# A transformer kernel on one core: a full weight slab ahead of the narrow one, and four smaller moves

## The chip, the cores and the metric

The kernel runs on one core of a Trainium2 chip. TensorE (PE) multiplies, VectorE (DVE), ScalarE (ACT) and GpSimd (POOL) do the rest, SyncE (SP) issues most DMAs. Each engine works off its own list of instructions in order; semaphores tie the lists together. The metric is the device time of one launch in microseconds; lower is better.

## The reference

One launch computes two transformer blocks one after the other on 256 rows of 1024 numbers, in float32:

```python
mod = silu(c) @ w_ada + b_ada                     # 6 vectors of 1024
h = rmsnorm(x, norm_mix_g) * (1 + sc_m) + sh_m
q, k, v, qi, ki, wi, u, ga, gb = split(h @ w_in)  # 5192 columns; ki 64, wi 8
y_attn = dsa_attention(q, k, v, qi, ki, wi) @ w_attn_proj   # top 64 keys by an index score
y_conv = conformer_conv(u, ...) @ w_conv_proj
x = x + g_m * ((sigmoid(ga) * y_attn + sigmoid(gb) * y_conv) @ w_out)
h = rmsnorm(x, norm_ffn_g) * (1 + sc_f) + sh_f
a, b = split(h @ w_ffn_in)
x = rmsnorm(x + g_f * ((silu(a) * b) @ w_ffn_out))
# second block: two attentions on h @ w_in_2, a cross attention to mem_2, a feed-forward
```

## The kernel before

**Weights.** A matmul of float32 is made of three in a rounded type: with w = w_hi + w_lo and a = a_hi + a_lo, it takes a_hi·w_hi, a_hi·w_lo and a_lo·w_hi (`mm3`, L527 to L529). SP loads weights in blocks of 1 MB into a ring of four (`load`, L390). A block is two pieces; ACT rounds each into w_hi (L1127) and DVE makes w_lo (L1551), again in a ring of four pieces. A slab of 512 output columns takes four pieces of 12 matmuls of 128x512, 48 in all. Numbers P_... count pieces, U_... count slabs (units), which alternate between PSUM banks 0, 1 and 2, 3. Before a block is loaded over an old one, SP waits until the last piece of the old one (`last_piece_of`) has its w_lo.

**The start.** POOL loads w_ada in 12 slabs of two 1 MB blocks (L478; the first four into `ada_raw` and `ada_start`); DVE multiplies each row group by silu(c) and sums (`ada_ops`, L1614 and L1617, eight instructions a slab). PE adds over the partitions (L618, one column each). With four slabs shift and scale of the first norm are known (L1636, `gain1` L1638). Between slabs DVE does the small steps of the first norm: the mean of the squares after slab 0 (`mean`, L1559), the scaled row group 0 after slab 1 (`rows0`, L1563), the copy of the transposed gain vectors and taps after slab 2 (L1630, L1631). POOL takes the power -1/2 (`rstd`, L484), ACT squares and scales row group 1. PE transposes the scaled rows (`turn`, L580), ACT and DVE apply gain and shift to two of four pairs of feature tiles each (L1155, L1576), then ACT rounds the four pairs into a_hi (L1161), then DVE makes a_lo (L1584).

**The first projection.** Its first slab is a narrow one, 72 columns (ki and wi; piece 0, block 0 of 288 KB), which waits for all four a_lo. Ten full slabs follow, pieces 1 on; DVE does slabs 4 to 11 of w_ada between their weight conversions, and the index scores, the top-64 search and the taps of the convolution. ki is copied twice side by side (`ki2`), transposed by PE after piece (1, 1) and moved by ACT.

**The norm before the first feed-forward** (`N_H2`): DVE adds the gated projection to x (L1952, L1957) by halves of 512 columns, ACT squares whole row groups (L1140), then mean, power, scaled rows, transposes and `features` as above.

**The second attention** ("b_"): 16 steps; at step n PE transposes probabilities (L733), issues the scores of step n + 2 (L724), does `mixed_step(n)`, a piece of 12 matmuls of another projection, then the values (L740). In `mixed_step` 5 and 6 it also transposes two groups of the memory's keys into bank 7 (L975); before the second it waits for DVE's copy of the first (`mem_kT`, L1602), which stands in DVE's step 8, the copy of the second in step 9.

## Time and profile before

| | us |
|---|---|
| runs of the kernel before (3) | 1026.27, 1028.21, 1029.89 |
| the profiled execution, its own time | 1027.91 |
| its span | 1026.1 |

| engine | busy us | share |
|---|---|---|
| PE matmul | 932.5 | 91% |
| PE weight load | 734.8 | 72% |
| DVE | 625.0 | 61% |
| ACT | 451.4 | 44% |
| POOL | 29.7 | 3% |

Stretches are in microseconds from the span's start. A timeline row has start and duration, engine, line of the program, operation, output<-input with shapes and the count of merged instructions; in brackets the idle time before it and what ended it. PEclk is the granted TensorE clock as a share of 2.4 GHz.

### The profile page before, as it was taken

How to read it: one execution, taken by the hardware profiler on the slowest of the kernel's cores; microseconds unless marked ns; L12 is line 12 of the kernel's file. 1: busy time of each engine (PE TensorE's matmuls, PEld its weight loads, DVE VectorE, ACT ScalarE, POOL GpSimd, SP SyncE). 2: the span in 40 equal slices, each digit the busy share in tenths (PEclk: the TensorE clock that was granted, in tenths of full speed). 3: DMA queues.
4: the chain of work that ended last, by engine and by line, in shares of the span. 5: the costliest groups of instructions: out<-in, count | busy, mean ns of one | idle time of the engine just before them, and what ended most of it. 6: DMA issues, size and time to landing. Idle time of an engine off the chain costs nothing.

```text
span 1026.1 us, 11727 instructions
## 1 busy us (share of the span) xinstructions
PE 932.5 (91%) x4133; PEld 734.8 (72%) x4133; DVE 625.0 (61%) x1015; ACT 451.4 (44%) x696; POOL 29.7 (3%) x41
## 2 busy tenths in 40 slices
PE   0599989998979999999999899797998899999997
PEld 0587544576868888887888678576777678888885
DVE  4868799857455555676766333577463555555544
ACT  1234222455354444543645434464254455555432
POOL 2101000000000000000000000000000000000000
PEclk9789999999889999999999989899999999999999
DMA  9959552446355655575554323145352346655541
GB/s 325 369 197 341 185 185 82 158 157 217 110 200 181 193 179 189 170 276 187 196 196 164 123 83 124 42 174 176 122 189 70 108 146 196 192 178 190 167 161 41
DMA packets 102853, 178.02 MB, mean 173 GB/s; under 512 B 6286, under 2 KB 52475, under 8 KB 102810
## 3 DMA queue, kind: packets, MB, share of 16 engines
q1 hardware_dynamic: 95994, 151.23, 44.9%
q0 software_dynamic: 6816, 26.22, 7.0%
q8 instruction: 26, 0.43, 0.2%
q14 instruction: 17, 0.14, 0.0%
HBM read 176.39 MB, written 1.05 MB: 173 GB/s over the span
## 4 chain that ended last, share of the span: by engine, by line
PE 76%; DVE 9%; issue 9%; ACT 3%; DMA 2%; POOL 0%; DVEq 0%; POOLq 0%; ACTq 0%
PE bank L527 19%; PE bank L529 18%; PE bank L528 18%; PE bank L879 9%; PE bank L560 3%; DVE conv_out L1763 2%; DVE ada_acc L1617 2%; ACT w_hi L1127 2%; DMA ada_raw<-in_w_ada 1%; PE bank L724 1%; DMA x_residual<-in_x 1%; PE bank L858 1%; PE bank L601 1%; PE bank L740 1%; DVE w_lo L1551 1%
## 5 line engine op out<-in xcount | busy, mean ns | idle before, releaser
L1551 DVE TENSOR_TENSOR w_lo<-raw_weights,w_hi 128x1024 fp32r<-128x1024 f32 (+1 forms) x259 | 315.0, 1222 | 283.1 <-ACT w_hi L1127 282.7
L1127 ACT ACTIVATE w_hi<-raw_weights 128x1024 fp32r<-128x1024 f32 (+1 forms) x259 | 272.4, 1058 | 334.4 <-PE bank L529 253.5
L527 PE MATMUL bank<-w_hi,a_hi 128*128 128x512 f32 (+1 forms) x792 | 322.2, 407 | 13.2 <-DVE a_lo L1584 5.6
L529 PE MATMUL bank<-w_hi,a_lo 128*128 128x512 f32 (+1 forms) x792 | 314.8, 397 | 0.0
L528 PE MATMUL bank<-w_lo,a_hi 128*128 128x512 f32 (+1 forms) x792 | 314.7, 397 | 0.0
L527 PEld LDWEIGHTS bank<-w_hi,a_hi 128*128 128x128 f32 x792 | 154.9, 196 | 49.1 <-issue 15.7
L529 PEld LDWEIGHTS bank<-w_hi,a_lo 128*128 128x128 f32 x792 | 154.6, 195 | 32.5
L528 PEld LDWEIGHTS bank<-w_lo,a_hi 128*128 128x128 f32 x792 | 155.2, 196 | 30.0 <-issue 0.2
L560 PE MATMUL bank<-raw_weights,feature_rows_early 128*128 128x512 f32 x144 | 68.0, 618 | 0.4 <-ACT z_projected L1201 0.4
L879 PE MATMUL bank<-w_hi,ff_hi 128*128 128x512 f32 x176 | 55.1, 394 | 0.8 <-DVE hidden_rows L2030 0.5
L879 PE MATMUL bank<-w_lo,ff_hi 128*128 128x512 f32 x176 | 54.3, 390 | 0.0
L879 PE MATMUL bank<-w_hi,ff_lo 128*128 128x512 f32 x176 | 54.2, 389 | 0.0
L1763 DVE SCALAR_TENSOR_TENSOR conv_out<-conv_in,conv_taps_T,conv_out 128x256 f32<-128x256 f32 x120 | 50.9, 475 | 0.0
L560 PEld LDWEIGHTS bank<-raw_weights,feature_rows_early 128*128 128x128 f32 x144 | 26.8, 195 | 32.0 <-issue 31.5
L1212 ACT ACTIVATE probabilities<-masked_scores,row_stats 128x128 f32<-128x128 f32 (+1 forms) x32 | 14.6, 455 | 59.8 <-DVE row_stats L1876 40.2
L879 PEld LDWEIGHTS bank<-w_hi,ff_hi 128*128 128x128 f32 x176 | 32.7, 188 | 8.6 <-DVE hidden_rows L2030 0.9
L879 PEld LDWEIGHTS bank<-w_hi,ff_lo 128*128 128x128 f32 x176 | 33.0, 188 | 7.0
L879 PEld LDWEIGHTS bank<-w_lo,ff_hi 128*128 128x128 f32 x176 | 33.0, 188 | 6.9
L1617 DVE SCALAR_TENSOR_TENSOR ada_acc<-ada_raw,row_stats,ada_acc 128x512 f32<-128x512 f32 x42 | 31.5, 750 | 3.2 <-DMA ada_raw<-in_w_ada 2.0
L527 PE MATMUL bank<-w_hi,mem_hi 128*128 128x512 f32 x64 | 26.3, 411 | 0.4 <-ACT z_projected L1235 0.4
L608 PE MATMUL bank<-constants,vector_rows 109*128 109x109 f32 x1 | 0.4, 416 | 28.2 <-DMA tap_rows<-in_w_dw 28.2
L529 PE MATMUL bank<-w_hi,mem_lo 128*128 128x512 f32 x64 | 25.7, 401 | 0.0
(244 smaller groups left out, 835.2 us busy)
## 6 DMA issues: line engine op xcount, KB each, us to landing
raw_weights<-in_w_in SPq DMA_DIRECT2D x40, 1024.0 KB, 5.1
raw_weights<-in_w_ffn_in SPq DMA_DIRECT2D x44, 512.0 KB, 4.7
raw_weights<-in_w_gate_up SPq DMA_DIRECT2D x44, 512.0 KB, 4.6
ada_raw<-in_w_ada POOLq DMA_DIRECT2D x12, 1024.0 KB, 8.1
raw_weights<-in_w_ffn_out SPq DMA_DIRECT2D x9, 1024.0 KB, 5.0
...
```

What stands on the lines that cost most here:

```text
L527: pe.matmul(ps, hi[:, kt, ts], wh, start=start, stop=False)
L528: pe.matmul(ps, hi[:, kt, ts], wl, start=False, stop=False)
L529: return pe.matmul(ps, lo[:, kt, ts], wh, start=False, stop=stop)
L560: last = pe.matmul(ps, f_h1[:, kt, t * P:(t + 1) * P], w, start=(kt == 0), stop=(kt == 2 * n - 1))
L601: last = pe.transpose(bank[b0 + g][:, kk * SEQ + t * P:kk * SEQ + (t + 1) * P], src[:, t, c:c + P], ident)
L724: pe.matmul(bank[4 + n % 2][:, 0:keys], q[half, h // 2, t * P:(t + 1) * P], k[half, h // 2, 0:keys], start=True, stop=True).then_inc(event ...
L879: o = pe.matmul(bank[out_bank(t, c)][:], lhs[:, kt, ts], w[:, c * W:(c + 1) * W], start=(kt == 0 and n == 0), stop=(kt == KF - 1 and n == 2))
L1127: act.activation(w_hi[:, slot, 0:m], raw[:, b % RAW, half * PIECE:half * PIECE + m], ACT.Copy)\
L1212: act.activation(p_work[:, n % 2, 0, 0:keys], s_work[:, n % 2, 0, 0:keys], ACT.Exp, scale=-1.0, bias=stat[:, 32 + n % 2:33 + n % 2], accum ...
L1551: dve.tensor_tensor(w_lo[:, slot, 0:m], raw[:, b % RAW, half * PIECE:half * PIECE + m], w_hi[:, slot, 0:m], ALU.subtract).then_inc(lo_read ...
L1617: o = dve.scalar_tensor_tensor(out=slot, in0=w, scalar=c, in1=slot, op0=ALU.mult, op1=ALU.add)
L1763: dve.scalar_tensor_tensor(out=conv_out[:, g, :], in0=conv_in[:, g, k:k + SEQ], scalar=taps[:, g, k:k + 1], in1=conv_out[:, g, :], op0=ALU ...
```

## The change

1. The first full slab of w_in (columns of u) becomes pieces 0 to 3 in blocks 0 and 1, and the narrow slab piece 4 in block 2. SP issues the loads after step 20 of w_ada's sums and not after 16. PE's first piece waits for its own pair of features only. ACT rounds two pieces before the features; DVE makes one residue of weights before them.
2. DVE takes the mean of the first norm after slab 1 of w_ada (before: slab 0), scales row group 0 after slab 2 (before: 1), and copies the vectors after slab 3 (before: 2), out of bank 3 and no longer 7. PE transposes the scaled rows before the vectors. The ki copies, transposes and move come one piece or more later.
3. `features`: ACT does pair 0 and rounds it, then pair 2, then rounds 1 to 3; DVE does pair 1, residue 0, pair 3, residues 1 to 3.
4. At N_H2 ACT squares halves of 512 columns as they come; DVE adds the two sums.
5. The table of constants is loaded in two parts: ident, ones and half ahead (264 of 1416 columns), the others after load 3; index scores and ln_mean wait for them.
6. Second attention: PE's key transposes in steps 5 and 8 (before 5 and 6), DVE's copies in steps 8 and 11 (before 8 and 9).

```diff
+    parts["half"] = np.full((P, KD), -0.5)
...
+P_FIRST, U_FIRST = 0, 0
+P_SMALL, U_SMALL = 4, 1
...
-    return (0, 0) if p == P_SMALL else (1 + (p - 1) // 2, (p - 1) % 2)
+    return (p // 2, p % 2) if p <= P_SMALL else (1 + (p - 1) // 2, (p - 1) % 2)
...
-    return 2 * b
+    return 2 * b + (b < 2)
@@ SP
-        sp.dma_start(const[:], const_dram[:]).then_inc(sem["const_landed"], 16)
+        early = cols["half"][1]
+        sp.dma_start(const[:, 0:early], const_dram[:, 0:early]).then_inc(sem["const_landed"], 16)
...
-        sp.wait_ge(ada_step, 16)
-        load(0, w2["w_in"].rearrange("(k p) n -> p k n", p=P)[:, :, C_KI:C_U], "small")
-        for s, c in enumerate(IN1_COLS):
+        sp.wait_ge(ada_step, 20)
+        for j in range(2):
+            load(j, slab_src(w2["w_in"], 4 * j, IN1_COLS[0]))
+        load(2, w2["w_in"].rearrange("(k p) n -> p k n", p=P)[:, :, C_KI:C_U], "small")
+        load(3, slab_src(w2["w_in"], 0, IN1_COLS[1]))
+        sp.dma_start(const[:, early:], const_dram[:, early:]).then_inc(sem["shapes_landed"], 16)
+        load(4, slab_src(w2["w_in"], 4, IN1_COLS[1]))
+        for s, c in enumerate(IN1_COLS[2:]):
             for j in range(2):
-                load(1 + 2 * s + j, slab_src(w2["w_in"], 4 * j, c))
+                load(5 + 2 * s + j, slab_src(w2["w_in"], 4 * j, c))
@@ PE
         pe.wait_ge(sem["const_landed"], 16)
+        turn(N_H1, xs_z)
         pe.wait_ge(small_landed, 16 * 12)
-        pe.transpose(bank[7][:, 0:V_ROWS], vec_rows[0:V_ROWS, :], ident[0:V_ROWS, 0:V_ROWS])
+        pe.transpose(bank[3][:, 0:V_ROWS], vec_rows[0:V_ROWS, :], ident[0:V_ROWS, 0:V_ROWS])
...
-        pe.wait_ge(sem["vec_copied"], 2)
-        turn(N_H1, xs_z)
...
         last.then_inc(sem["ada_reduced"], 1)
+        for j in range(4):
+            piece(P_FIRST + j, U_FIRST, j, 4, norm=N_H1)
+
+        pe.wait_ge(lo_ready, P_SMALL + 1)
         pe.wait_ge(sem["mod_copied"], 1)
-
-        pe.wait_ge(lo_ready, P_SMALL + 1)
-        pe.wait_ge(nt["lo"], 4 * F_OF[N_H1] + 4)
+        pe.wait_ge(sem["vec_copied"], 2)
...
-        for s in range(6):
+        for s in range(1, 6):
...
-                if (s, j) == (1, 1):
+                if (s, j) == (1, 2):
...
-            if 5 <= n < 7:
-                g = n - 5
+            if n in (5, 8):
+                g = n // 8
@@ ACT, features
+            affine(0)
+            rounded(0)
+            affine(2)
+            for g in range(1, 4):
+                rounded(g)
...
-        conv(P_SMALL)
+        conv(P_FIRST, 2)
         act.wait_ge(sem["gains"], 1)
         features(N_H1, f_h1, gain1, modT[:, 0:8])
-        conv(P_IN1, 3)
...
+        conv(P_FIRST + 2, 2)
...
+        conv(P_SMALL, 4)
+        slab_out(P_FIRST + 3, U_FIRST, IN1_COLS[0], ACT.Copy)
+        conv(P_SMALL + 4)
...
-        sumsq(N_H2, x, xs_u, updated(U_OUT1 + 2), {1: (P_FI1 + 1, 1)})
+        def half_squares(t, c, done):
+            act.wait_ge(acc_free[t], U_OUT1 + c + 1)
+            o = act.activation(xs_u[:, t, c * W:(c + 1) * W], x[:, t, c * W:(c + 1) * W], ACT.Square, scale=1.0 / 32,
+                               accum_out=d_stat[:, 28 + 2 * c + t:29 + 2 * c + t])
...
+        half_squares(0, 0, False)
+        half_squares(1, 0, False)
+        half_squares(0, 1, True)
+        conv(P_FI1 + 1)
+        half_squares(1, 1, True)
@@ DVE, features
+            affine(1)
+            residue(0)
+            affine(3)
+            for g in range(1, 4):
+                residue(g)
...
-            if s == 0:
+            if s == 1:
                 mean(N_H1)
-            elif s == 1:
+            elif s == 2:
                 rows0(N_H1, x, xs_z)
-            elif s == 2:
-                dve.wait_ge(sem["vec_turned"], 1)
...
+        dve.wait_ge(sem["vec_turned"], 1)
...
-        features(N_H1, f_h1, gain1, modT[:, 0:8], P_SMALL)
-        conv(P_IN1, 4)
+        conv(P_FIRST)
+        features(N_H1, f_h1, gain1, modT[:, 0:8])
+        conv(P_FIRST + 1, 3)
...
+            dve.wait_ge(sem["shapes_landed"], 16)
...
+        conv(P_SMALL)
...
-                if (s, k) == (0, 1):
+                if (s, k) == (1, 0):
...
-        mean(N_H2)
+        dve.wait_ge(nt["sumsq"], TT * (N_H2 + 1))
+        dve.scalar_tensor_tensor(out=stat[:, 2:4], in0=d_stat[:, 28:30], scalar=EPS, in1=d_stat[:, 30:32],
+                                 op0=ALU.add, op1=ALU.add).then_inc(nt["mean"], 1)
...
-            if 8 <= n < 10:
-                g = n - 6
+            if n in (8, 11):
+                g = 2 + n // 11
```

## Rows read from the trace of the kernel before

**Rows 1.** The page: busy time of the engines, GB/s in 40 slices, the chain.

```profile
PE 932.5 (91%) x4133; PEld 734.8 (72%) x4133; DVE 625.0 (61%) x1015; ACT 451.4 (44%) x696; POOL 29.7 (3%) x41
...
GB/s 325 369 197 341 185 185 82 158 157 217 110 200 181 193 179 189 170 276 187 196 196 164 123 83 124 42 174 176 122 189 70 108 146 196 192 178 190 167 161 41
...
PE 76%; DVE 9%; issue 9%; ACT 3%; DMA 2%; POOL 0%; DVEq 0%; POOLq 0%; ACTq 0%
```

**Rows 2.** Stretches: length, busy PE, PEld, DVE, ACT, POOL, clock, DMA share, GB/s.

```profile
46.30:56.50 10.20, 10.19 (x48) 10.20 (x49) 3.36 (x3) 1.96 (x3) 0.00 (x0) 0.50 0.67 240
56.50:61.30 4.80, 4.80 (x13) 3.82 (x13) 2.38 (x3) 1.18 (x2) 0.00 (x0) 0.50 0.20 35
61.30:69.80 8.50, 8.50 (x39) 6.98 (x38) 6.73 (x12) 3.18 (x3) 0.75 (x1) 1.00 0.55 187
69.80:120.00 50.20, 49.48 (x221) 36.23 (x219) 40.15 (x71) 19.99 (x34) 5.25 (x7) 1.00 0.77 279
120.00:200.00 80.00, 75.73 (x234) 37.56 (x234) 79.09 (x224) 21.10 (x54) 2.04 (x3) 0.96 0.44 146
```

**Rows 3.** Timeline of the start.

```profile
19.74 0.17 DVE L1559 TENSOR_SCALAR row_stats<-row_stats 128x2 f32<-128x2 f32 x1 [6.31 <-ACT scaled_rows_early L1140]
...
20.33 5.54 DVE L1617 SCALAR_TENSOR_TENSOR ada_acc<-ada_start,row_stats,ada_acc 128x512 f32<-128x512 f32 x7
...
36.51 3.12 DVE L1617 SCALAR_TENSOR_TENSOR ada_acc<-ada_start,row_stats,ada_acc 128x512 f32<-128x512 f32 x4 [0.65 <-DMA ada_start<-in_w_ada]
...
41.19 1.90 DVE L1576 TENSOR_SCALAR feature_rows_early<-bank,gain_h,modulation_T 128x256 f32<-128x256 f32 x4
...
43.67 2.50 DVE L1584 TENSOR_TENSOR a_lo<-feature_rows_early,a_hi 128x512 fp32r<-128x512 f32 x4
...
46.31 0.40 PE L527 MATMUL bank<-w_hi,a_hi 128*128 128x72 f32 x1 [5.58 <-DVE a_lo L1584]
```

**Rows 4.** Chain of waits: start, duration, 16 transposes at full clock.

```profile
492.88 1.75 PE bank L590 x16
```

**Rows 5.** DMAs of two tiles: ada_start (0 to 60), raw_weights (issued 25.9 to 27.5).

```profile
L478 POOL DMA_DIRECT2D ada_start<-in_w_ada x4: 748/750/797, 2.9 to 26.2; - x4
...
DMA to landing us min/median/max: 7.6/10.5/15.5
...
DMA to landing us min/median/max: 8.4/17.4/21.6
```

**Rows 6.** The one-column matmuls (timeline), and the stretch in which they end.

```profile
36.63 4.10 PE L618 MATMUL bank<-constants,ada_acc 128*128 128x1 f32 x32
...
40.00:41.00 1.00, 0.73 (x7) 0.65 (x6) 0.20 (x2) 0.00 (x0) 0.00 (x0) 0.92 1.05 391
```

**Rows 7.** Timeline at the norm before the feed-forward, and the stretch behind it.

```profile
283.76 1.22 DVE L1551 TENSOR_TENSOR w_lo<-raw_weights,w_hi 128x1024 fp32r<-128x1024 f32 x1
...
287.33 3.65 PE L580 MATMUL bank<-constants,scaled_rows 128*128 128x128 f32 x16 [4.94 <-ACT scaled_rows L1146]
...
289.31 0.99 DVE L1576 TENSOR_SCALAR feature_rows<-bank,gain_h,modulation_T 128x256 f32<-128x256 f32 x2 [1.39 <-PE bank L580]
...
292.72 0.77 PE L527 MATMUL bank<-w_hi,a_hi 128*128 128x512 f32 x1 [1.74 <-issue]
...
292.70:296.80 4.10, 4.08 (x10) 3.23 (x11) 2.86 (x4) 1.51 (x3) 1.53 (x2) 0.50 0.12 14
```

**Rows 8.** Timeline of PE in the second attention, and the stretch after the stall.

```profile
589.42 0.48 PE L724 MATMUL bank<-kbT,qbT 64*128 64x128 f32 x2
...
597.71 0.48 PE L724 MATMUL bank<-kbT,qbT 64*128 64x128 f32 x2
...
602.89 0.63 PE L975 MATMUL bank<-constants,z_projected 128*128 128x128 f32 x4 [1.74 <-DVE mem_kT L1602]
...
611.05 0.48 PE L724 MATMUL bank<-kbT,qbT 64*128 64x128 f32 x2
...
604.00:611.00 7.00, 7.00 (x19) 5.05 (x17) 0.43 (x2) 1.93 (x5) 0.00 (x0) 0.51 0.37 141
```

48 lines of the change are left out of this document (20 added, 28 removed).

## The prediction, made before the change was run

> **What bounds the kernel now.** I read the page first. TensorE's matmuls are busy 91% of the span and make 76% of the chain that ended last [rows 1], so time leaves this kernel in two ways only: the places where TensorE stands still, and those where it runs at the lower of its two clock levels. The table of stretches comes next, for the granted clock. From 46.3 to 61.3 us TensorE is busy without a gap, but at a granted clock of 0.50, which is 1.2 GHz; later the clock is 1.00, which is 2.4 GHz [rows 2]. Two thirds of that slow stretch is the narrow slab of 72 columns, 48 matmuls from 46.31 to about 56.5 us [rows 2, 3]. In the three touched places the timeline shows what ended the idle time before TensorE's next instruction. At the start the last thing late is VectorE's residues a_lo: the last four end at 46.17 and the first matmul is at 46.31. Before them lie the gains at about 41.15, and before those the sum over w_ada, whose last half slab waits for a DMA until 36.51 [rows 3]. At the norm ahead of the first feed-forward TensorE waits 1.74 us from its last transpose (290.98) to its first matmul (292.72) [rows 7]. In the second attention it waits 1.74 us for a copy of VectorE, and then runs seven us at half clock [rows 8].
>
> **Part 1, the start of the first stage.** The mean of the rows moves behind w_ada's slab 1. VectorE now stands idle 6.31 us before that mean, until ScalarE's squares end at 19.71 [rows 3]; slab 1 (a first product of 0.5 and seven sums of 5.54 together, 6.1 us) fills that hole. Its second half can't begin before ada block 3 has landed: of the four blocks in ada_start one took 15.5 us [rows 5], and since block 2 was issued first, at 2.9, and blocks 6 and 7 were not waited for that long, I take block 3, at about 19.2. So slab 1 ends at 22.4, and the mean comes then and not at 19.74; GpSimd's power follows to 23.3. Slab 2 ends at 28.7, the scaled row 0 at 29.5. GpSimd's queue has the power ahead of ada blocks 6 and 7, so they are issued at about 23.3 and 24.1 (block 7 today: issued at 26.2, landed at 36.51 [rows 3, 5]). That is earlier, but block 7 stands behind block 6 and all engines' rings carry 325 to 369 GB/s in these two slices of the page [rows 1], so I give it only what the removed traffic gives: of the constants' 1416 columns 1152, 576 KB, no longer come ahead, at 369 GB/s 1.6 us, shared with the other queue. I take 1.1 us: landed at 35.4, slab 3 done at 35.4 + 3.1 = 38.5, gains at 38.5 + 1.5 = 40.0 in place of 41.15. Bounds: no gain, and 3 us. The two copies of the transposed vectors (0.55 us) come behind slab 3 now, but TensorE's sums take 1.1 us there, which covers them.
>
> From the gains on VectorE first makes the residue of weight piece 0 (1.22 us, the row of 283.76 in [rows 7]), then its affine pair (0.95, half of 1.90 [rows 3]), then residue 0 (0.65, a quarter of 2.50 [rows 3]). TensorE starts at 40.0 + 1.25 + 0.95 + 0.7 + 0.2 of handovers = 43.1 us, where today it needs all four residues and starts at 46.3. ScalarE must have rounded pieces 0 and 1 before its own affine pairs: block 0, now 1 MB and not 0.29 MB, is issued at about 25.5. Today's four loads, issued from 25.9 on, land after 8.4 to 21.6 us, median 17.4 [rows 5]; the 8.4 is the small one. The new first one carries 3.6 times the bytes of the old first; I take 11 to 13 us, 36.5 to 38.5, just early enough. The later pieces are ready in time: their residues end at about 47.0, 48.2 and 49.4, and a piece at half clock lasts 5.1 us.
>
> The order of the slabs: today 10.2 us of narrow slab and 4.8 us of full slab run at 0.50 [rows 2]. In the new order the full slab carries the clock up. The clock rose 4.1 us after the first dense matmul at the second norm [rows 7] and 4.8 us after 56.5 [rows 2]; I take 4.8. The full slab is 48 matmuls of 512 columns, 0.427 us apart in the slow stretch, 0.227 us in the fast one (13 in 4.80 us and 39 in 8.50 us [rows 2], whose first and last overlap the edges): 4.8 us give 11.2 of them, the other 36.8 take 8.35 us, end at 56.3. The narrow slab at full clock: 48 instructions, by the nearest row of full-clock instructions of one weight load each (16 transposes in 1.75 us [rows 4], 0.109 each): 5.25 us, end at 61.5. Today both slabs are done at 61.3 + 8.4 = 69.7. That would be 8.2 us.
>
> But will the clock stay up in the narrow slab? The 32 matmuls of one column, without a gap from 36.63 to 40.73, ended with the clock falling (0.92 in the us from 40 to 41) though the engine was busy [rows 6], and 72 columns did not raise it in 10.2 us [rows 2]. So I count one more slow stretch, as long as the one after the stall in the second attention (7.0 us at 0.51 [rows 8]), which costs half, 3.4 us. Part 1: 8.2 - 3.4 = **4.8 us**; bounds 2 and 9.
> The Trainium skill (TensorE: Matmul & The Clock Gate, "What's actually happening") ties the lower clock to idleness and the higher to being busy; by that rule the narrow slab, which has no gaps, keeps the clock and part 1 gives the full 8.2 us. The row of one-column matmuls speaks against it.
>
> Does it carry? VectorE is busy 79.1 of 80 us between 120 and 200 [rows 2], so there it is the bound. Its work there starts when TensorE's logits come, and it has idle time before, 10.0 of 50.2 us from 69.8 to 120 [rows 2], so it moves with TensorE. The first wait on the late constants comes with the index scores, tens of us after they land. The moved ki transposes find their copies done.
>
> **Part 2, the norm before the feed-forward.** The last square is of 512 columns and not 1024, but VectorE's conversion from 283.76 to 284.98 [rows 7] stands ahead of the mean and doesn't move: 0 to 0.1 us. Pair by pair, residue 0 no longer waits behind affine 3: affine 1 ends at 290.3, residue 0 at 290.97, and TensorE's transposes at 290.98 [rows 7]. TensorE starts at 291.1 in place of 292.7: **1.6 us**. If the clock rises at the same moment as today, the time won is worked off at half speed, 0.8 us; if it rises earlier with the start, up to 2.5. Residues 1 to 3 (0.65 us each) end long before TensorE asks for them.
>
> **Part 3, the keys of the memory.** TensorE's second group of transposes moves from step 6 to step 8, VectorE's copy from step 9 to 11. Today TensorE at step 6 waits for the copy that VectorE makes at its step 8, behind scores that TensorE issued just before [rows 8]. Two steps with four transposes take 8.29 us (589.42 to 597.71); the two from 597.71 to 611.05 take 13.34 [rows 8]. The difference, **5.05 us**, is the 1.74 us stall and half of the 7 us at 0.51. In the new place the copy is done some 6 us before it is asked for. Lower bound: 1.74 us, if the clock does not fall here in the other runs; upper 5.2.
>
> **Sum** against the profiled execution's own time, 1027.91 us (span 1026.1, 1.8 around it; the median of the runs is 1028.21, 0.3 above): 4.8 + 1.6 + 5.05 = 11.45, gives **1016.5 us**.
>
> **Rivals.** (a) The clock stays up in the narrow slab: 3.4 us more, 1013. For: it has no idle gaps. Against: [rows 6]. (b) The start is DMA-bound: block 0 lands like the middle of today's four, 17.4 us after its issue [rows 5], at 42.9. ScalarE must round pieces 0 and 1 (2.1 us) before its affine pair (1.0) and its rounding (0.55), then comes residue 0 (0.65): a landing at L gives a start at L + 4.3, here 47.2, 4.1 us later than I sum: 1020.6. (c) The time won at the start is lost again where VectorE is full, between 120 and 200: 1021.3. For: 79.1 of 80 us; against: its idle time before 120. (d) The change doesn't do what it says in part 3: a wait at step 8 replaces that at step 6, or the clock falls there anyway: 5 us less, 1021.5. Against: the 6 us of slack. (e) Slower: block 0 lands so late that it holds everything. By the same rule all 11.45 us are gone at a start of 54.5, and 3.1 us more (slower by 0.3%) at 57.6, so at L = 53.3, 28 us after the issue, where the longest of today's four took 21.6 [rows 5].
>
> **Chances.** Forecast 45%, (a) 20%, (b) 14%, (c) 9%, (d) 9%, (e) 3%. The likeliest gives 1016.5. The range takes in (a) with the upper bound of part 2 and one slow-clock stretch less elsewhere (1010.5), and (c) and (d) (1021.5), since each later stall may or may not pull the clock down. 0.3%, about what a measurement of this kernel can tell from no change, is 3.1 us: faster by more 0.94, within 0.03, slower 0.03.
>
> **What would show it.** In the changed profile: the mean at 22 to 23 us; first dense matmul at about 43; clock 1.00 from about 48; narrow slab at 0.11 us a matmul and a fall of the clock in or behind it; both first slabs done at 61 to 65; TensorE waiting less than 0.2 us between the last transpose and the first matmul at the second norm; no wait before the second group of key transposes and steps of 3.9 to 4.3 us throughout. It is wrong if ScalarE waits for block 0 beyond 39, if the stretch from 120 to 200 grows by what the start won, or if waits of TensorE appear that today has not.

## The result

| us | before | after |
|---|---|---|
| median of the runs | 1027.24 (4 runs, 1021.87 to 1029.89) | 1009.15 (4 runs, 1008.59 to 1010.20) |
| the profiled execution, its own time | 1027.91 | 1008.59 |
| its span | 1026.1 | 1006.8 |
| mean granted clock over the span | 0.964 | 0.974 |

After to before is 0.983, with a 95% interval of 0.980 to 0.986. The change makes the kernel faster, as forecast, by 1.7%. But it gives 19.3 us in the profiled executions where the sum had 11.45; the median of 1009.15 lies 1.4 us below the range.

**The page of the kernel after**, busy time and chain, which answer to [rows 1]:

```profile
PE 921.2 (91%) x4133; PEld 726.0 (72%) x4133; DVE 624.3 (62%) x1015; ACT 452.1 (45%) x700; POOL 29.8 (3%) x41
...
PE 78%; issue 8%; DVE 7%; DMA 4%; ACT 2%; POOL 1%; DVEq 0%; POOLq 0%; ACTq 0%
```

The count of matmuls is the same, but their busy time is 11.3 us less (932.5 to 921.2): the same work ran longer at the upper clock level. The other 8 us are, in the main, waits that went: 4.2 us by which TensorE starts its first slab earlier, 1.74 at the norm and 1.74 at the keys.

**The start, timeline of after** (it answers to [rows 3]):

```profile
18.36 3.11 DVE L1648 SCALAR_TENSOR_TENSOR ada_acc<-ada_start,row_stats,ada_acc 128x512 f32<-128x512 f32 x4 [1.75 <-DMA ada_start<-in_w_ada]
...
21.39 0.16 DVE L1588 TENSOR_SCALAR row_stats<-row_stats 128x2 f32<-128x2 f32 x1
...
22.48 1.55 POOL L485 DMA_DIRECT2D ada_start<-in_w_ada  x2
...
24.33 15.88 SPq L392 DMA_DIRECT2D raw_weights<-in_w_in  x4
...
33.41 3.12 DVE L1648 SCALAR_TENSOR_TENSOR ada_acc<-ada_start,row_stats,ada_acc 128x512 f32<-128x512 f32 x4 [1.30 <-DMA ada_start<-in_w_ada]
...
37.65 2.00 ACT L1136 ACTIVATE w_hi<-raw_weights 128x1024 fp32r<-128x1024 f32 x2 [13.95 <-DMA raw_weights<-in_w_in]
38.69 0.17 DVE L1667 SCALAR_TENSOR_TENSOR gain_h<-modulation_T,vectors_T 128x8 f32<-128x8 f32 x1
...
39.56 1.00 ACT L1165 ACTIVATE feature_rows_early<-bank,modulation_T,gain_h 128x256 f32<-128x256 f32 x2
...
41.25 0.69 DVE L1609 TENSOR_TENSOR a_lo<-feature_rows_early,a_hi 128x512 fp32r<-128x512 f32 x1 [0.23 <-ACT a_hi L1171]
...
42.09 0.77 PE L534 MATMUL bank<-w_hi,a_hi 128*128 128x512 f32 x1 [3.65 <-DVE a_lo L1609]
```

The last half slab of w_ada starts at 33.41 and not 36.51, the gains stand at 38.86, and TensorE starts at 42.09. Block 0 lands at 37.65, 13.3 us after its issue. ScalarE rounds its two pieces until 39.56 and is 0.7 us late for the gains; on VectorE, which has its own work until then, 0.23 us of that arrive as a wait for a_hi.

**Stretches of after** (columns as in [rows 2]): the start, the norm ahead of the feed-forward, the second attention where the keys' stall was, and the third attention.

```profile
42.10:46.20 4.10, 4.10 (x10) 3.24 (x11) 4.10 (x7) 3.59 (x6) 0.00 (x0) 0.50 1.12 348
46.20:55.00 8.80, 8.80 (x41) 7.25 (x39) 7.68 (x10) 2.81 (x3) 0.75 (x1) 1.00 1.04 388
55.00:60.00 5.00, 5.00 (x46) 5.00 (x45) 3.91 (x5) 2.03 (x3) 0.68 (x1) 0.98 1.03 372
60.00:63.50 3.50, 3.50 (x12) 2.97 (x12) 1.44 (x2) 1.30 (x3) 0.07 (x1) 0.53 1.04 384
...
282.80:285.10 2.30, 2.27 (x6) 1.82 (x6) 2.24 (x5) 2.30 (x5) 0.00 (x0) 0.50 0.00 0
285.10:293.00 7.90, 7.90 (x36) 6.55 (x35) 4.14 (x4) 3.12 (x4) 1.53 (x2) 1.00 0.71 240
594.00:602.00 8.00, 8.00 (x42) 6.25 (x41) 3.43 (x7) 4.47 (x10) 0.00 (x0) 1.00 0.28 86
625.20:656.90 31.70, 23.82 (x119) 17.29 (x118) 19.73 (x71) 17.74 (x50) 0.00 (x0) 0.95 0.21 67
```

The full slab carries the clock up 4.1 us after it begins; the narrow slab (from 55.00) takes 0.11 us a matmul, and the clock falls at its end. At the norm the clock rises 2.3 us after the first matmul, before it took 4.1 [rows 7]. In the second attention it stays at 1.00 where it was 0.51 [rows 8].

**The norm, timeline of after** (it answers to [rows 7]):

```profile
279.17 3.65 PE L587 MATMUL bank<-constants,scaled_rows 128*128 128x128 f32 x16 [4.76 <-ACT scaled_rows L1155]
...
281.15 0.99 DVE L1602 TENSOR_SCALAR feature_rows<-bank,gain_h,modulation_T 128x256 f32<-128x256 f32 x2 [1.39 <-PE bank L587]
...
282.06 0.68 DVE L1609 TENSOR_TENSOR a_lo<-feature_rows,a_hi 128x512 fp32r<-128x512 f32 x1
...
282.85 0.77 PE L534 MATMUL bank<-w_hi,a_hi 128*128 128x512 f32 x1
```

The last transpose ends at 282.82, the first matmul starts at 282.85: no wait.

**Where the time went.** A stage lasts from the start of one instruction to that of the next named one, the same instructions in all timelines; here they are as differences, the first from the span's start; the last one ends at GpSimd's first power of the last norm, 9.9 us before the span's end. The last columns are second executions of both kernels, profiled later (labels before_2 and after_2, below).

| stage, us | before | after | gain | forecast | before_2 | after_2 |
|---|---|---|---|---|---|---|
| start, to the first a_hi of the first attention | 225.26 | 217.56 | 7.70 | 4.8 | 227.40 | 219.10 |
| to the first transpose of the norm | 62.07 | 61.61 | 0.46 | 0 to 0.1 | 61.74 | 60.65 |
| to the transposes of the memory's rows | 146.61 | 143.96 | 2.65 | 1.6 | 146.43 | 143.64 |
| to the second attention | 130.38 | 130.45 | -0.07 | 0 | 130.31 | 130.47 |
| second attention, to the first score of the third | 77.04 | 71.68 | 5.36 | 5.05 | 77.03 | 72.99 |
| third attention | 34.34 | 31.61 | 2.73 | 0 | 34.34 | 32.44 |
| its output projection, to the next norm | 68.14 | 67.71 | 0.43 | 0 | 68.15 | 66.46 |
| the rest | 272.36 | 272.29 | 0.07 | 0 | 272.32 | 272.36 |
| sum | 1016.20 | 996.87 | 19.33 | 11.45 | 1017.72 | 998.11 |

Two terms are larger than forecast, and one stage that the diff doesn't touch is 2.7 us shorter. These are the questions for the experiments. Gains and losses below are against the runs of the changed kernel, 1009.15, unless another kernel is named. These ran in another round than the kernels of the experiments. The kernel before ran in every round, with medians from 1026.98 to 1027.68 us, so differences under 1 us between rounds say nothing.

### The profile page after: what moved, and what is told of

The parts are those of the page before. It is cut to its first block, busy times and chain, and to the rows that moved or that the text cites. A ratio compares the mean times of both kernels' runs of the same rounds, so it can differ in the third digit from the quotient of the medians.

```text
span 1006.8 us, 11736 instructions
## 1 busy us (share of the span) xinstructions
PE 921.2 (91%) x4133; PEld 726.0 (72%) x4133; DVE 624.3 (62%) x1015; ACT 452.1 (45%) x700; POOL 29.8 (3%) x41
## 3 DMA queue, kind: packets, MB, share of 16 engines
HBM read 176.39 MB, written 1.05 MB: 176 GB/s over the span
## 4 chain that ended last, share of the span: by engine, by line
PE 78%; issue 8%; DVE 7%; DMA 4%; ACT 2%; POOL 1%; DVEq 0%; POOLq 0%; ACTq 0%
PE bank L534 19%; PE bank L536 18%; PE bank L535 18%; PE bank L888 9%; PE bank L567 4%; PE bank L732 1%; DVE ada_acc L1648 1%; DMA ada_start<-in_w_ada 1%; DMA raw_weights<-in_w_in 1%; ACT w_hi L1136 1%; PE bank L867 1%; PE bank L748 1%; DMA ada_raw<-in_w_ada 1%; DVE conv_out L1794 1%; PE bank L608 1%
## 5 line engine op out<-in xcount | busy, mean ns | idle before, releaser
L1580 DVE TENSOR_TENSOR w_lo<-raw_weights,w_hi 128x1024 fp32r<-128x1024 f32 x259 | 314.9, 1222 | 271.7 <-ACT w_hi L1136 271.2
L1136 ACT ACTIVATE w_hi<-raw_weights 128x1024 fp32r<-128x1024 f32 x259 | 272.4, 1057 | 337.1 <-PE bank L536 253.2
L534 PE MATMUL bank<-w_hi,a_hi 128*128 128x512 f32 (+1 forms) x792 | 317.6, 401 | 9.6 <-DVE a_lo L1609 3.6
L536 PE MATMUL bank<-w_hi,a_lo 128*128 128x512 f32 (+1 forms) x792 | 310.6, 392 | 0.0
L535 PE MATMUL bank<-w_lo,a_hi 128*128 128x512 f32 (+1 forms) x792 | 310.6, 392 | 0.0
L534 PEld LDWEIGHTS bank<-w_hi,a_hi 128*128 128x128 f32 x792 | 151.7, 192 | 44.6 <-issue 11.2
L536 PEld LDWEIGHTS bank<-w_hi,a_lo 128*128 128x128 f32 x792 | 151.1, 191 | 31.9
L535 PEld LDWEIGHTS bank<-w_lo,a_hi 128*128 128x128 f32 x792 | 151.4, 191 | 29.5 <-issue 0.2
L567 PEld LDWEIGHTS bank<-raw_weights,feature_rows_early 128*128 128x128 f32 x144 | 26.7, 194 | 32.1 <-issue 31.6
L587 PE MATMUL bank<-constants,scaled_rows_early 128*128 128x128 f32 x16 | 3.6, 423 | 28.3 <-DVE scaled_rows_early L1592 28.3
```

Source lines behind the costliest of these rows:

```text
L534: pe.matmul(ps, hi[:, kt, ts], wh, start=start, stop=False)
L535: pe.matmul(ps, hi[:, kt, ts], wl, start=False, stop=False)
L536: return pe.matmul(ps, lo[:, kt, ts], wh, start=False, stop=stop)
L567: last = pe.matmul(ps, f_h1[:, kt, t * P:(t + 1) * P], w, start=(kt == 0), stop=(kt == 2 * n - 1))
L1136: act.activation(w_hi[:, slot, 0:m], raw[:, b % RAW, half * PIECE:half * PIECE + m], ACT.Copy)\
L1580: dve.tensor_tensor(w_lo[:, slot, 0:m], raw[:, b % RAW, half * PIECE:half * PIECE + m], w_hi[:, slot, 0:m], ALU.subtract).then_inc(lo_read ...
```

## The experiments

### One part alone

My theory was that three parts add up; the rival that one of them carries most. Three kernels take one part each, a fourth leaves out only the order of the slabs.

```diff
# keys_only, on the kernel before
-            if 5 <= n < 7:
-                g = n - 5
+            if n in (5, 8):
+                g = n // 8
...
-            if 8 <= n < 10:
-                g = n - 6
+            if n in (8, 11):
+                g = 2 + n // 11
# feats_only, on the kernel before (DVE; ACT alike)
-            for g in (1, 3):
...
+            affine(1)
+            residue(0)
+            affine(3)
+            for g in range(1, 4):
+                residue(g)
# start_only: the kernel after, with keys, half squares and the order of pairs at N_H2 undone
# narrow_first: the kernel before with everything but the new order of the slabs
#   and of their loads (narrow slab first, waits for all four a_lo, loads after step 16)
```

> The kernel before with only part 3 (second group of key transposes in step 8, copies in steps 8 and 11). Theory A (the gain is the 1.74 us stall and the 7 us at half clock behind it): 5.1 us less than before in the profile, six steps of the second attention at 3.9 to 4.3 us, no wait before the second key transposes; the median 3 to 6 us lower. Rival B (the clock would have fallen in the other runs anyway or not at all, the profile of before was an unlucky one): only 1.7 to 2.5 us. Rival C (a wait at step 8 takes the stall's place): under 1 us. Separately: from the third attention on, the two profiles differ by 2.7 us in stages that the change does not touch, because the clock was low there for 10 us before and for 2.6 us after. If those stretches are chance, this kernel has one or the other length; if they hang on what was moved, this kernel shows about the short one only when the whole change does.

> The kernel before with only the new order of affine, rounding and residue (both norms with shift). The narrow slab still waits for all four residues, so at the start nothing is to be gained: 0 to 0.3 us. At the norm before the feed-forward the first dense matmul comes 1.7 us sooner after the first transpose (3.7 us and not 5.4). Theory A (the start of the dense work also decides when the clock rises): the slow stretch behind it is 2 to 4 us long, and the stage gains 1.7 to 2.7 us. Rival B (the clock rises at the same moment whatever the start): the stage gains 0.8 us. In the median 1 to 3 us.

> The changed kernel with parts 3 and the norm before the feed-forward put back (keys in steps 5 and 6, old order of its features, squares of whole rows), so the start alone is changed. Theory A (the start won 7.7 us in the profile: 4.2 by the earlier first matmul, the rest because full slabs and not the narrow one run at the low clock, less one short slow stretch behind the narrow slab): 7 to 9 us less than before, and the milestones up to the first attention's end come 7 to 8.5 us earlier, the same distance there as at the end of the narrow slab. Rival B (what is won at the start is partly lost where VectorE is full, from 120 to 200 us): the distance shrinks on the way, 3 to 6 us left.

> All of the change but the order of the two slabs: the narrow slab is first again and waits for all four residues; mean, row 0 and vector copies one block back, constants in two parts, features pair by pair, halves of squares and keys are as in the changed kernel. Theory A (most of the start's 7.7 us is the order: 10.2 us of narrow slab at half clock): against the changed kernel 5 to 7 us slower, the clock stays at 0.50 through the whole narrow slab and rises 3.5 to 5 us into the full one. Rival B (the gain at the start comes from the earlier sums over w_ada and the smaller load of constants): under 3 us slower than the changed kernel.

| kernel | median (range) | to before, 95% | start | norm to memory | 2nd attention | 3rd |
|---|---|---|---|---|---|---|
| keys_only | 1017.34 (1016.85 to 1018.85) | 0.991 [0.988, 0.994] | 224.02 | 146.34 | 71.97 | 31.73 |
| feats_only | 1017.75 (1016.35 to 1020.04) | 0.991 [0.988, 0.994] | 224.82 | 144.02 | 73.67 | 32.45 |
| start_only | 1019.87 (1015.98 to 1021.31) | 0.993 [0.990, 0.996] | 218.73 | 146.60 | 77.01 | 34.38 |
| narrow_first | 1015.58 (1014.95 to 1016.55) | 0.989 [0.986, 0.992] | 224.25 | 143.90 | 71.62 | 31.58 |

The kernel before ran at 1027.45 beside them (12 runs). The stages are from one profiled execution each. Keys_only and feats_only gained more than expected (10.1 and 9.7 us where 3 to 6 and 1 to 3 were expected); start_only (7.6) and narrow_first (6.4 slower than the changed kernel) came as their theories A had it.

Three things follow. Each mechanism sits where the prediction put it: only the kernels with the new slab order start early, only those with the new order of pairs shorten the stage behind the norm (by 2.6 to 2.7 us), and the second attention is shortest, at 72 us or less here, without the stall. Second, the parts don't add: 10.1 + 9.7 + 7.6 is 27.4 us, and all together give 18.1. Third, feats_only gains nearly four times the 2.6 us of its stage: in its profile the stall is there, but the clock doesn't fall behind it. Row of the stall and the stretch behind it in feats_only:

```profile
599.63 0.63 PE L975 MATMUL bank<-constants,z_projected 128*128 128x128 f32 x4 [1.74 <-DVE mem_kT L1614]
```

```profile
600.00:607.00 7.00, 7.00 (x36) 5.45 (x35) 1.27 (x3) 3.48 (x7) 0.00 (x0) 1.00 0.46 151
```

The same 1.74 us as in [rows 8], followed by 1.00 and not 0.51. Whether the clock falls here is thus not settled by the stall alone: an edit elsewhere, or chance, can win those 3.5 us too, and then part 3 can't win them again. The stages say where the excess lies. In the profiles the three single parts win 27.6 us together and the whole change 19.3. Of the 8.3 us between them 3.1 are in the second attention (8.5 against 5.4), 1.7 in the third (4.5 against 2.7) and 3.0 in the output projection behind it (3.4 against 0.4): keys_only and feats_only each win these three stages, and they can be won once.

Narrow_first also says what the start lives on: mean, vectors and constants moved, with the narrow slab first and the loads after step 16 as before, give 1.0 us there (225.26 to 224.25), not the 7.7 of the whole. Even that 1.0 is not shown to be a gain: keys_only, whose start is that of the kernel before, has 224.02. Its last half slab of w_ada starts at 35.46 us, as late as in the four executions with the old start (35.36 to 36.51) and 2 us later than in after.

### The keys put back into the changed kernel

```diff
# keys_undone, on the kernel after
-            if n in (5, 8):
-                g = n // 8
+            if 5 <= n < 7:
+                g = n - 5
...
-            if n in (8, 11):
-                g = 2 + n // 11
+            if 8 <= n < 10:
+                g = n - 6
```

> The changed kernel with only the key transposes and copies of the second attention put back (transposes in steps 5 and 6, copies in steps 8 and 9). Theory: the stall of 1.74 us is back, and with it a stretch at 0.50 in the second attention and a longer one in the third, whose stage (first scores of the second memory half to the next turn) took 34.34 us before and 31.61 after. Then the attention stage is 77.0 us again (from 71.68), the next stage 34.3 (from 31.61), and the time is 1009.2 + 5.3 + 2.7 = 1017.2. Rival: the next stage's gain belongs to chance, that is to where the slow stretches happen to fall in an execution, and not to this part: then it stays at 31.5 to 32.5 and the time is 1013.7 to 1014.5, or 1010.9 to 1012 if the clock does not fall at the stall.

1015.73 us (0.988 [0.984, 0.992]), but the six runs lie at 1011.54, 1012.26, 1014.00, 1017.47, 1017.69 and 1017.89. The profiled one is the 1017.69: 77.40 us for the second attention and 34.39 for the third, as the theory had it. The stall's row and the stretches behind it, then the third attention:

```profile
592.63 0.63 PE L984 MATMUL bank<-constants,z_projected 128*128 128x128 f32 x4 [1.75 <-DVE mem_kT L1633]
```

```profile
594.00:600.00 6.00, 6.00 (x14) 4.29 (x15) 0.43 (x2) 1.58 (x4) 0.00 (x0) 0.50 0.40 151
631.10:665.50 34.40, 26.51 (x117) 19.18 (x117) 19.68 (x71) 17.67 (x50) 0.00 (x0) 0.85 0.18 62
```

Since the single times disagreed by 6 us I looked at more executions of the same kernels:

> The changed kernel with the keys put back, a second profiled execution. Single times of it were 1011.5 to 1017.9 us. Theory: where the execution takes about 1017.5 the attention stage takes 77.0 to 77.4 and the next 34.4 (as in the first, 77.40 and 34.39); where it takes 1011.5 to 1014, the clock does not fall at the stall, the stage takes about 73.5 and the next 31.6 to 32.5. Rival: any pairing.

> The changed kernel with the keys put back, a third profiled execution, with the same expectations as the second: 77.0 to 77.4 and 34.4 us in an execution of about 1017.5, or 73.5 and 31.6 to 32.5 us in one of 1011.5 to 1014. Rival: any pairing.

> The kernel before, once more, for a second profiled execution. Its attention stage took 77.04 us with the clock falling at the stall of the keys, the next stage 34.34. Theory (the fall at the stall is a matter of where it meets the clock's course, and the longer slow time in the third attention follows from it): either 77.0 and 34.3 again, or, if the clock does not fall at the stall, 73.6 and 31.6 to 32.5 in an execution of 1018 to 1023 us. Rival (the two are unrelated): any pairing of the two values.

> The changed kernel, a second profiled execution. In its first the slow stretches were 46.8 us long in sum, shorter than in the kernels that differ from it in a norm only (51.2 us with the halves undone). Theory: lengths vary by execution, so this one shows single stretches of 6.8 us where the first showed 3.4 or the other way, stages that differ by 0.8 to 1.7 us, and a sum within 3 us of 1008.6. Rival: the stretches belong to the kernel's own order of work, and the second execution shows the same ones within 0.3 us.

| execution | its time | clock behind the stall | 2nd attention | 3rd |
|---|---|---|---|---|
| keys_undone | 1017.69 | 0.50 for 6.8 us | 77.40 | 34.39 |
| keys_undone_2 | 1011.36 | 1.00 | 73.66 | 32.41 |
| keys_undone_3 | 1013.76 | 0.50 for 3.4 us | 76.56 | 32.41 |
| before | 1027.91 | 0.50 for 6.8 us | 77.04 | 34.34 |
| before_2 | 1029.39 | 0.50 for 6.8 us | 77.03 | 34.34 |
| start_only | 1021.31 | 0.50 for 6.8 us | 77.01 | 34.38 |

The same program, three times, and the clock fell behind the same stall fully, half, or not at all. Over all profiled executions of this study it fell there in five of the seven with the stall (in feats_only it did not either), and in none of the eleven without it. The row of the stall in the execution where it did not fall, with the stretches of the second and the third attention:

```profile
593.08 0.63 PE L984 MATMUL bank<-constants,z_projected 128*128 128x128 f32 x4 [1.75 <-DVE mem_kT L1633]
```

```profile
554.70:628.40 73.70, 67.93 (x318) 52.58 (x317) 28.56 (x60) 31.92 (x70) 0.00 (x0) 0.98 0.34 115
628.40:660.80 32.40, 24.52 (x117) 17.77 (x117) 19.69 (x71) 17.73 (x50) 0.00 (x0) 0.89 0.18 65
```

The theory held for the pairing at its ends, not in the middle: 34.3 to 34.4 us in the third attention came in all four executions with a full fall behind the stall, and in none of the fourteen others of this study (31.6 to 32.5), the one with a half fall among them. The waits of TensorE in the third attention are the same wherever I listed them (this is the list of waits of after, its columns total, times and longest):

```profile
PE bank L1011 <- DVE probabilities L2182: 6.2, 4, 1.8
PE bank L1018 <- ACT probabilities_T L1490: 0.9, 1, 0.9
PE bank L1001 <- DVE component_stats L2165: 0.8, 1, 0.8
```

So the 2.7 us of this untouched stage are clock and nothing else: it is granted 0.85 of full speed in the long case (10.2 us at 0.50), 0.89 in the middle one (6.8 us) and 0.95 in the profile of after (3.4 us). The pairing, four of four against none of fourteen, ties it to a full fall in the stage before; by what way, I can't say, and no run here shows it.

After_2 bears out that the lengths of the slow stretches belong to the execution. Behind the narrow slab it has 6.8 us at 0.50 where the first had 3.4, at the start of the second attention 6.8 and not 3.4, later 3.4 and not 6.8; the execution takes 1009.81 us, 1.2 more than the first. The stretch behind the narrow slab in after_2, and the third attention:

```profile
60.00:67.00 7.00, 7.00 (x20) 5.65 (x21) 2.38 (x3) 2.10 (x4) 0.00 (x0) 0.54 0.96 341
...
626.80:659.30 32.50, 24.62 (x119) 17.80 (x118) 19.72 (x71) 17.71 (x50) 0.00 (x0) 0.89 0.19 65
```

### Does the narrow slab pull the clock down?

The prediction counted one slow stretch for it (3.4 us) and gave rival (a), no fall, 20%. The edit runs the narrow slab's matmuls twice:

```diff
# narrow_twice, on the kernel after, narrow slab only
+                for _ in range(2):
                     <the 12 matmuls of the piece, 72 columns each>
```

> The changed kernel with the 48 matmuls of the narrow slab issued twice into the same banks, same result, so 5.4 us more work at full clock. Theory A (72 columns a weight load do not count as activity enough for the clock): the clock falls inside the narrow slab and stays low to its end, the second half of it runs at half speed, the two copies take 14 to 18 us and the kernel is 8 to 12 us slower. Rival B (the clock falls only where the engine idles, the fall seen in the changed kernel came from its last part and the change of slabs): 5.4 us slower, the clock at 1.00 through both copies.

1018.65 us (1017.98 to 1019.83), 9.5 more, as theory A had it (8 to 12). The stretches of narrow_twice from 58.6 us on:

```profile
58.60:60.00 1.40, 1.40 (x9) 1.40 (x8) 0.00 (x0) 0.00 (x0) 0.75 (x1) 0.51 1.06 391
60.00:70.00 10.00, 10.00 (x49) 10.00 (x48) 0.00 (x0) 0.00 (x0) 0.00 (x0) 0.50 0.40 149
70.00:75.70 5.70, 5.70 (x17) 4.64 (x17) 2.37 (x3) 1.30 (x3) 0.00 (x0) 0.50 0.20 39
```

TensorE is busy all of 10 us from 60 to 70 and its clock is at 0.50 throughout, 17 us in all until the matmuls of 512 columns have brought it back at 75.7. In after the fall comes at 59.84, with the narrow slab nearly over (60.4), so that there mainly the slab behind it pays. So rival (a) is refuted, and so is rival B of this run: matmuls of 72 columns without a gap do go with a fall of the clock, and they don't raise it again. The Trainium skill (TensorE: Matmul & The Clock Gate, "What's actually happening") ties the lower clock to idleness; these rows, busy and slow at once, disagree, and the measurement decides.

### The halves of the squares, and matmuls of constants in the waits

Halves_undone puts ScalarE's whole-row squares and the old mean back into N_H2. Fill_norm leaves the changed kernel as it is and lets TensorE multiply constants by constants, into a bank that nothing reads yet, while it waits for the norm. Fill_all does it at five places: around the sums at the start, at the norm, ahead of the transposes of the outputs of two attentions, and after the last piece of the input. These matmuls are added work; no output depends on them.

```diff
# halves_undone
-        half_squares(0, 0, False)
...
+        sumsq(N_H2, x, xs_u, updated(U_OUT1 + 2), {1: (P_FI1 + 1, 1)})
# fill_norm
+        def filler(n, b, src):
+            for _ in range(n):
+                pe.matmul(bank[b][:], ones, src, start=True, stop=True)
...
+        filler(5, 4, const[:, 0:W])
         turn(N_H2, xs_u)
# fill_all, further places
+        filler(1, 0, ada_acc[:, 0, :])      # and three more around the first norm's sums
...
+        filler(4, 4, const[:, 0:W])         # ahead of the transposes of two attentions' outputs
...
+            filler(3, 6, const[:, 0:W])     # after the last input piece
```

> The changed kernel with ScalarE's squares of whole rows and the old mean at the norm before the feed-forward. Theory A (VectorE's weight residue stands ahead of the mean and hides the shorter square): the time from the first attention's output to the norm's transposes is within 0.2 us of the changed kernel's 61.61 us. Rival B (the halves themselves win what the stretch has gained, 62.0 to 62.1 us without them and 61.5 to 61.6 with them in the five profiles so far): 62.0 us here. Either way too little for the median to show, 0 to 0.5 us.

> The changed kernel with five matmuls of 512 columns on constants, whose result nobody reads, on TensorE in the 5 us in which it waits for the scaled rows of the norm before the feed-forward. Theory A (TensorE's idle time lets the clock fall, and what a stage loses to the low clock is bought by that wait): the clock stays at 1.00, the 16 transposes take 1.8 us and not 3.65, the stretch from the first transpose to the memory's transposes 141.0 us and not 144.0, kernel 2 to 4 us faster. Rival B (the fill-in delays the transposes, or the clock falls for another reason): no gain, or up to 1 us slower.

> As fill_norm, with such matmuls also at the start (one before the last sum over w_ada, two and a half between the sums and the first full slab), before the transposes of both merged projections (four each, waits of 4.2 us) and in the 3.7 us wait at the second attention's start. Theory A: each of these stretches runs at full clock, 8 to 14 us faster than the changed kernel. Rival B (the fill-ins collide with what comes free or end too late): under 4 us faster, with the first full slab starting after 42.6 us.

Beside 1026.98 for the kernel before (7 runs): halves_undone 1009.71 (0.983 [0.981, 0.985]), fill_norm 1010.08 (0.983 [0.982, 0.985]), fill_all 1005.45 (0.979 [0.977, 0.980]).

The halves are worth nothing that the runs can tell. In the profiles TensorE's wait for the scaled rows is 4.76 us with them ([4.76 <-ACT scaled_rows] above) and 4.94 without, in the kernel before [rows 7] and in halves_undone alike: 0.18 us, where the prediction had 0 to 0.1. The stage to the norm's transposes answered neither theory: it took 60.82 us in halves_undone, where 61.4 to 61.8 or 62.0 were expected. There its slow stretch is 3.4 us long and in after 6.8, and that hides the 0.18.

Fill_norm keeps the clock up at the norm, as its theory A said, and yet gains nothing in the runs, as its rival B said. Its rows at the norm:

```profile
279.71 1.94 PE L591 MATMUL bank<-constants,scaled_rows 128*128 128x128 f32 x16 [0.47 <-ACT scaled_rows L1160]
...
282.88 0.47 PE L534 MATMUL bank<-w_hi,a_hi 128*128 128x512 f32 x1 [1.24 <-issue]
```

```profile
286.00:296.00 10.00, 10.00 (x46) 8.29 (x45) 5.20 (x5) 4.76 (x6) 1.32 (x2) 1.00 0.89 304
```

The transposes take 1.94 and not 3.65 us, since the clock is up, but the first matmul waits for its residue all the same: VectorE sets its start now, and 1.24 us of wait come back. What is saved is the slow time after it: the stage from norm to memory is 142.40 us long, in place of 143.96 in after and 143.64 in after_2 (141.0 was expected). But the next stage, to the second attention, is 1.2 us longer, 131.65 against 130.47 in after_2. The reason stands in TensorE's only wait of that stage, first in after_2, then in fill_norm:

```profile
455.94 1.95 PE L646 MATMUL bank<-ada_acc,constants 128*128 128x512 f32 x4 [0.68 <-DVE ada_acc L1648]
...
455.85 1.96 PE L650 MATMUL bank<-ada_acc,constants 128*128 128x512 f32 x4 [1.87 <-DVE ada_acc L1653]
```

TensorE comes 1.3 us earlier and then waits 1.2 us longer for VectorE's late sums over w_ada. What the norm gave is lost there.

Fill_all is 3.7 us faster than the changed kernel, within its rival B (under 4, with the first slab after 42.6 us: it starts at 44.97) and far from theory A (8 to 14). From 50 us on it has 20.5 us at 0.50 in its profile where after has 37.6; ahead of that its clock is not recorded. But its fillers at the start cost more than they gave: the first a_hi of the first attention comes at 220.93, 3.4 us later than in after.

> The kernel with matmuls of constants in every wait of TensorE that was filled (1005.45 us in its runs), but without those at the start of the launch, with which the first slab came later (the first residues of the attention at 220.93 in place of 217.56 us). The matmuls that remain stand ahead of the transposes of three norms and after the last input piece, and change no output. Theory: the start is that of the changed kernel, the rest that of the filled one: 1005.45 - 3.4 = 1002.1, faster than both kernels. Rival: what the filled start cost was paid back later by a slow stretch less, and without it the time is 1004.5 to 1006.

```diff
# fill_late, on fill_all
-        filler(1, 0, ada_acc[:, 0, :])      # all four at the start go
```

1004.84 us (six runs, 1002.01 to 1005.71; 0.978 [0.975, 0.982]), faster than both kernels, 4.3 us under the changed one. But against fill_all it gives 0.6 us and not the 3.4 of the theory; the rival was nearer. Its start is at 219.00, and so 1.9 us earlier than fill_all's, not 3.4, since behind its narrow slab the clock was down for 6.8 us, as in after_2; further on it has a slow stretch at the start of the second attention (3.4 us) that fill_all has not, and from the memory's transposes on fill_all is 1.4 us faster.

### What sets the start: loads and constants

> The changed kernel with its weight loads issued after step 16 of the sum over w_ada, as in the kernel before, and not after step 20. In the changed kernel block 0 lands at 37.65 us, 13.3 after its issue, and ScalarE's affine pair starts at 39.56 although the gains are there at 38.86. Theory A: the block lands as long after its issue as now, so before 35 us; the affine pair starts with the gains, and all after it comes 0.7 us earlier: 1008.5. Theory B: the block shares the queues with the last two blocks of w_ada, these land later (now 33.41), and the gains with them, by 1 to 3 us: 1010 to 1012.

> The changed kernel with the whole table of constants loaded ahead, the second part (576 KB) right after the first. The prediction gave the split 1.6 us of traffic and took 1.1 us of it for the start. If that holds, the last blocks of w_ada and block 0 land 1.1 to 1.6 us later, the first matmul of 512 columns comes at 43.2 to 43.7 in place of 42.09, and the time is 1010.3 to 1010.8. Rival: the queues have room before 20 us, nothing lands later, and the time is 1009.2; the first matmul stays within 0.3 us of 42.09.

```diff
# load_early, on the kernel after
-        sp.wait_ge(ada_step, 20)
+        sp.wait_ge(ada_step, 16)
# const_whole, on the kernel after: the second part of the table loads right behind the first
+        sp.dma_start(const[:, early:], const_dram[:, early:]).then_inc(sem["shapes_landed"], 16)
```

Load_early 1010.48 us (1009.41 to 1012.05, 0.984 [0.981, 0.988]), const_whole 1011.44 us (1010.80 to 1011.87, 0.985 [0.982, 0.988]), both beside 1027.68 for the kernel before (11 runs). Timeline of load_early at the start:

```profile
32.48 2.00 ACT L1136 ACTIVATE w_hi<-raw_weights 128x1024 fp32r<-128x1024 f32 x2 [8.83 <-DMA raw_weights<-in_w_in]
32.49 0.49 DVE L1645 TENSOR_SCALAR ada_acc<-ada_start,row_stats 128x512 f32<-128x512 f32 x1 [4.36 <-DMA ada_start<-in_w_ada]
...
36.03 3.11 DVE L1648 SCALAR_TENSOR_TENSOR ada_acc<-ada_start,row_stats,ada_acc 128x512 f32<-128x512 f32 x4 [0.70 <-DMA ada_start<-in_w_ada]
...
44.40 0.76 PE L534 MATMUL bank<-w_hi,a_hi 128*128 128x512 f32 x1 [3.33 <-DVE a_lo L1609]
```

Block 0 is there at 32.5, 5.2 us earlier, as theory A says, and it doesn't help, as theory B says: the last two blocks of w_ada land at 32.5 and 36.0 (after: 29.3 and 33.4), and TensorE starts 2.3 us later. In load_early the weights are issued from 21.43 us on, ahead of these two blocks of w_ada (22.43), in after behind them (24.33 and 22.48). W_ada is the one that is waited for. Narrow_first, which issues its loads after step 16 as well, has the last half slab as late (35.46). So this is one of the things that the new start wins, and the prediction had not named it: it took the move from step 16 to step 20 as a delay for block 0 only.

Const_whole starts at 44.23, 2.1 us later than after (expected 1.1 to 1.6). The first of these two waits after doesn't have; the second is as long there:

```profile
22.57 0.68 DVE L1645 TENSOR_SCALAR ada_acc<-ada_raw,row_stats 128x512 f32<-128x512 f32 x1 [1.18 <-DMA ada_raw<-in_w_ada]
...
35.47 3.11 DVE L1648 SCALAR_TENSOR_TENSOR ada_acc<-ada_start,row_stats,ada_acc 128x512 f32<-128x512 f32 x4 [1.30 <-DMA ada_start<-in_w_ada]
```

The 576 KB push a block of w_ada back by 1.2 us, and the sum runs 1.3 us behind. The two blocks of w_ada that set the start are issued at 22.23 us, no later than in after (22.48), and still VectorE gets them at 31.32 and 35.47, both 2.1 us later.

How sure are these two prices? Ten profiled executions have the start of the changed kernel: after, after_2, start_only, halves_undone, fill_norm, fill_late, narrow_twice and the three of keys_undone. Their last half slab of w_ada starts at 33.22 to 34.08 us and their first matmul of 512 columns at 41.97 to 43.06. After (33.41, 42.09) is near the early end. Against all ten, load_early delays the half slab by 2.0 to 2.8 us and const_whole by 1.4 to 2.3, and TensorE by 1.2 to 2.4. So both delays are real, but that 576 KB cost more than the 1.6 us of their bytes is not shown. Nor is the kernel's time for load_early: its runs overlap those of the changed kernel (from 1009.41 against up to 1010.20); those of const_whole lie above (from 1010.80).

A part of the spread is TensorE's own. Its 32 one-column matmuls took 4.10 us in before [rows 6], and in before_2, the same program:

```profile
36.63 6.83 PE L618 MATMUL bank<-constants,ada_acc 128*128 128x1 f32 x32
```

They start at the same moment, 36.63, and the gains wait for the last of them, so before_2's first matmul of the narrow slab comes at 49.03 and not 46.31, 2.7 us later. The small matmuls at the start are on the critical path, and their pace differs between executions.

## Why the prediction was right or wrong

The three mechanisms were right, and so was the direction. Two steps failed. The sum put the weight loads' move from step 16 to step 20 at nothing for w_ada, and so had the last half slab of w_ada at 35.4 us where it starts at 33.41. And it put every stage that the diff doesn't touch at 0, where the third attention alone gave 2.73 us.

The range has a slip too. Its lower end, 1010.5, is rival (a), 1013.1, less 0.9 for the upper bound of part 2, less one slow stretch elsewhere. That leaves 1.7 us for this stretch, but part 1 and part 3 of the same prediction priced one at 3.4 to 3.5. At that price the lower end is 1008.7 to 1008.8, and 1009.15 lies above it.

**Part 1, 4.8 forecast, 7.70 measured (6.2 between before and after_2, 8.3 between before_2 and after_2).** Over all profiles the stage takes 217.56 to 219.69 us in the nine executions with the new start and nothing added at it, with 219.00 in the middle, and 224.02 to 227.40 in the four with the old one. After has the shortest of the nine, so of the 7.7 a part is luck: from middle to middle it is 6.0. The chain of reasoning held step by step: the mean at 21.39 (forecast 22 to 23), blocks 6 and 7 issued at 22.5 and 23.3 (23.3 and 24.1), first matmul of 512 columns at 42.09 (43.1), full slab over at 55.0 (56.3), narrow slab at 0.11 us a matmul, with a fall of the clock at its end. Three terms were mis-sized. TensorE starts 1.0 us earlier: the last half slab starts at 33.41 and not 35.4, since I priced the constants at 1.1 us (1.4 to 2.3 by const_whole) and the loads' later issue at nothing (2.0 to 2.8 by load_early). The two don't add up: from before to after the half slab comes 3.1 us earlier in all. Of these 2.0 us 0.8 are lost between the last sum and the gains (2.33 us and not 1.5), where the last eight one-column matmuls run at half clock for 1.86 us and I had 1.1 for them; the chain from the gains to TensorE takes 3.2 us, as forecast (3.1). The clock rises after 4.1 us, not 4.8, worth 0.35 us. And the new slow stretch is 3.4 us long in the first profile, 1.7 us of loss and not 3.4. After_2 has it at 6.8 us, as forecast; there the term is right and 1.4 us of the difference are left, the two other terms. So the range of that term is 1.7 to 3.4 us, and the prediction held only its upper end, which is the more frequent one: of the twelve executions with the full slab ahead and a single narrow one, seven have 6.8 us and five 3.4. Rival (b) has its mechanism but not its size: block 0 does come late for ScalarE, by 0.7 us, and 0.23 us of it reach VectorE, not 4.

**It carries.** The start's gain is 7.8 us at 80 us, at the same matmul of the third full slab, and still 7.7 at 217 us, past the stretch in which VectorE is full (120 to 200 us). Rival (c) is refuted. Row of that stretch in after, with VectorE at 75.4 of 80 us:

```profile
120.00:200.00 80.00, 75.39 (x242) 39.52 (x241) 75.38 (x213) 22.65 (x57) 1.29 (x2) 0.96 0.45 148
```

**Part 2, 1.6 forecast, 2.65 measured.** The wait of 1.74 us is gone, as forecast, with 0.03 left. The prediction named what would decide over more or less, the moment at which the clock rises, and gave up to 2.5 us; it rose 2.3 us after the first matmul and not 4.1. In all executions with the new order of pairs and no added matmuls the stage takes 143.0 to 144.1 us, in all without it 146.3 to 146.6: 2.3 to 3.6 us, so the forecast should have stood at or above its upper bound of 2.5.

**Part 3, 5.05 forecast, 5.36 measured** in the first pair of profiles, 4.04 in the second. The stall went and none came at step 8. The slow time behind it isn't a constant of the kernel, as its lower bound (1.74 us) allowed for: put back into the changed kernel the stall cost full, half or no fall. Rival (d) is refuted.

**What the sum left out.** The third attention, 2.73 us (1.90 in the second pair), and up to 1.7 us in the stage behind it. The prediction said of the untouched stages that nothing changes, except that "each later stall may or may not pull the clock down" and took that into the range as one stretch less. The size was wrong: before has 71.7 us at 0.50 in its profile (35.8 us of loss), after 47.8 (23.9), the last few us of the span left out. (The expectation of after_2 says 46.8, which is 1.0 too low.) Of the 11.9 us between them the start has 3.4, the norm 1.7, the keys 3.4 and the third attention 3.4. The sum had, by clock alone, 1.5 at the start (10.2 less 5.25 for the narrow slab, less 3.4), 3.5 at the keys and none at the norm or in the third attention. The step that failed is that each slow stretch was costed beside the edit that touches it, while a full fall in the second attention goes with about 2 to 2.7 us more in the third; why it does stays open. Together 19.3 = 11.45 + 2.9 (start) + 1.05 (norm) + 0.3 (keys) + 3.6 (0.5 at halves, 2.7 third attention, 0.4 behind it).

**Other ways to be wrong, looked at.** The waits that could have been new are not there: from 63 to 120 us, with the index scores and the moved ki transposes, TensorE waits 0.7 us in all, for an eviction of ScalarE, and nothing waits for the late constants. The slower rival (e) needed block 0 at 53.3; it came at 37.65, and in the thirteen profiled executions with the new order never later than 38.8.
